# Bias tables written to DRAM once instead of once per query, and read by one overlapping read in the weights' queue

## What is computed

```python
# first block, 8 heads, causal T5 buckets
bias = rel_bias[_t5_bucket(jnp.maximum(dist, 0))]
logits = logits + bias.astype(jnp.float32)
# second block, 8 heads, a clipped relative table
bias = rel_table[:, jnp.clip(rel, -REL_CLIP, REL_CLIP) + REL_CLIP]
sc = sc + bias[:, None].astype(jnp.float32)
# second block, 4 heads, T5 buckets of both signs
bias = t5_table[:, t5_bucket(key_pos[None, :] - q_pos[:, None])]
sc = sc + bias[None, :, None].astype(jnp.float32)
```

## Time and profile before

| | |
|---|---|
| median of 3 runs | 1163.42 us (1161.92 to 1164.56) |
| span of the profiled execution | 1164.8 us |
| TensorE matmul busy | 1100.0 us, 94% |
| VectorE busy | 667.0 us, 57% |
| ScalarE busy | 555.4 us, 48% |
| GpSimd busy | 195.8 us, 17% |
| DRAM read, written | 184.94 MB, 4.98 MB |

### The profile page before, as it was taken

The page is one execution under the profiler, slowest core; times in us unless marked ns, Lnnn a source line. Parts: engine busy times, 40 slices in busy tenths (PEclk is TensorE's granted clock), DMA queues, the critical chain, the costliest instruction groups (busy, mean ns, idle before and its releaser), DMA issues.

```text
span 1164.8 us, 22065 instructions
## 1 busy us (share of the span) xinstructions
PE 1100.0 (94%) x8802; PEld 1077.8 (93%) x8802; DVE 667.0 (57%) x772; ACT 555.4 (48%) x755; POOL 195.8 (17%) x234
## 2 busy tenths in 40 slices
PE   8737699999999999999999999999999999999998
PEld 6736699999999999999999999999999999999998
DVE  4032789756587666445864444575666577544343
ACT  4121355983465444445653334454656455333343
POOL 2000011011332112103241121110000042311110
PEclk7858799999999999999999999999999999999999
DMA  6655444566467664465667644676334545865363
GB/s 212 103 117 108 135 145 127 175 211 203 141 176 216 181 181 132 140 189 193 195 172 203 182 126 136 194 236 211 115 114 142 179 145 146 219 184 167 110 191 104
DMA packets 292291, 190.93 MB, mean 164 GB/s; under 512 B 6703, under 2 KB 288866, under 8 KB 292226
## 3 DMA queue, kind: packets, MB, share of 16 engines
q1 hardware_dynamic: 286942, 183.38, 53.0%
q10 hardware_dynamic: 5284, 6.62, 3.7%
HBM read 184.94 MB, written 4.98 MB: 163 GB/s over the span
## 4 chain that ended last, share of the span: by engine, by line
PE 78%; DMA 8%; DVE 5%; ACT 4%; issue 2%; POOL 1%; ACTq 1%; SPq 0%; DVEq 0%
PE bank L1581 48%; PE bank L1561 7%; PE bank L1563 7%; PE bank L1562 7%; DMA raw<-in_w_in 4%; DMA table<-table 3%; DVE wl L1073 2%; ACT wh L474 2%; DVE page_y L1099 2%; POOL xl L955 1%; PE bank L1804 1%; PE bank L1647 1%; ACTq L551 1%; PE bank L1859 1%; PE bank L1639 1%
## 5 line engine op out<-in xcount | busy, mean ns | idle before, releaser
L1073 DVE TENSOR_TENSOR wl<-raw,wh 128x2048 fp32r<-128x2048 f32 (+3 forms) x211 | 403.1, 1911 | 328.8 <-ACT wh L474 325.7
L474 ACT ACTIVATE wh<-raw 128x2048 fp32r<-128x2048 f32 (+3 forms) x212 | 336.2, 1587 | 270.5 <-PE bank L1581 120.2
L1581 PE MATMUL bank<-xh,wh 128*128 128x256 f32 x1552 | 445.1, 287 | 7.5 <-DVE page_g L1445 4.1
L1581 PE MATMUL bank<-xl,wh 128*128 128x256 f32 x1584 | 445.5, 285 | 1.2 <-POOL xl L955 1.2
L1581 PE MATMUL bank<-xh,wl 128*128 128x256 f32 x1552 | 441.4, 285 | 0.0
L1581 PEld LDWEIGHTS bank<-xh,wh 128*128 128x128 f32 x1552 | 300.7, 194 | 9.8 <-DVE wl L1073 8.6
L1581 PEld LDWEIGHTS bank<-xl,wh 128*128 128x128 f32 x1584 | 304.7, 194 | 2.1 <-POOL xl L955 1.6
L1581 PEld LDWEIGHTS bank<-xh,wl 128*128 128x128 f32 x1552 | 300.6, 194 | 0.0
L1561 PE MATMUL bank<-hh,wh 128*128 128x256 f32 x768 | 218.7, 285 | 1.7 <-ACT page_y L680 1.6
L1563 PE MATMUL bank<-hh,wl 128*128 128x256 f32 x768 | 217.3, 283 | 0.0
L1562 PE MATMUL bank<-hl,wh 128*128 128x256 f32 x768 | 217.3, 283 | 0.0
(11 more groups left out here) (229 smaller groups left out, 975.4 us busy)
## 6 DMA issues: line engine op xcount, KB each, us to landing
raw<-in_ffn_w_in SPq DMA_DIRECT2D x88, 512.0 KB
raw<-in_w_in SPq DMA_DIRECT2D x24, 1024.0 KB
raw<-in_w_up SPq DMA_DIRECT2D x48, 512.0 KB
raw<-in_w_mix_in SPq DMA_DIRECT2D x20, 1024.0 KB
raw<-in_ffn_w_out SPq DMA_DIRECT2D x32, 448.0 KB
raw<-in_w_down SPq DMA_DIRECT2D x24, 512.0 KB
raw<-in_ffn_w_out SPq DMA_DIRECT2D x16, 512.0 KB
raw<-in_w_attn_br SPq DMA_DIRECT2D x4, 1024.0 KB
```

The source lines that it names most:

```text
L474: act.activation(wh[:, u % RING, 0:w], raw[:, u % RING, 0:w], ACT.Copy).then_inc(rounded, 1)
L1073: dve.tensor_tensor(wl[:, s, 0:w], raw[:, s, 0:w], wh[:, s, 0:w].bitcast(F32), ALU.subtract).then_inc(rest, 1)
L1581: ins = mm(lin[group(u) % 3][:, s * T:(s + 1) * T], w, (low if j == 1 else high)[:, t0 + k, :], start=(k == 0 and j == 0), stop=(k == K - ...
```

## The change

The queries of each block of 128 are kept in reverse order from the projection to the output of the attention. With query 127-p in partition p, its bias begins p values into the table's row, so partition p, head h, key t needs the word at p + 384 h + t: one read with a partition step of one word, over rows that overlap, from a table that is in DRAM once.

```diff
-        table1 = nc.dram_tensor("table1", (8, P, REL), F32).ap()
+        table1 = nc.dram_tensor("table1", (8, REL), F32).ap()
...
+            def shifted(tab, nh):
+                return bass.AP(tab.tensor, tab.offset, [[1, P], [REL, nh], [1, T]])
...
+                if name == "V":
+                    sp.wait_ge(table_out[0], 16)
+                    sp.dma_start(bias8[:, :, :], shifted(table1, 8)).then_inc(bias_in[0], 16)
+                    sp.wait_ge(clip_ready, 1)
+                    sp.dma_start(table2, clip_table).then_inc(table_out[1], 16)
...
             load(U["RI1"], gates(1))
+            sp.wait_ge(table_out[1], 16)
+            sp.wait_ge(logit_done, 6)
+            sp.dma_start(bias8[:, :, :], shifted(table2, 8)).then_inc(bias_in[1], 16)
...
+                if name == "WO":
+                    sp.wait_ge(table_out[2], 16)
+                    sp.wait_ge(lru_m2, 2)
+                    sp.dma_start(bias4[:, :, :], shifted(table3, 4)).then_inc(bias_in[2], 16)
...
-            act.activation(kidx[0:72, :], lin[0][0:72, 0:T], ACT.Copy).then_inc(read_a, 1)
-
+            act.activation(kidx[0:64, :], lin[0][0:64, 0:T], ACT.Copy)
+            act.activation(by_half(widx), backwards(lin[0][64:72, 0:T]), ACT.Copy).then_inc(read_a, 1)
+            act.wait_ge(read_a, 1)
+            act.dma_start(kidx[64:128, :], kidx[0:64, :]).then_inc(ki_twice, 16)
             act.wait_ge(tab_mm, 1)
-            act.activation(table[:, :], turn_bank[0:8, 0:REL], ACT.Copy).then_inc(tab_sb, 1)
-            act.wait_ge(tab_sb, 1)
-            act.dma_start(table1, per_query(table[:, :])).then_inc(tab_out, 16)
+            act.activation(table[:, 0, :], turn_bank[0:8, 0:REL], ACT.Copy).then_inc(tab_sb, 1)
+            act.wait_ge(tab_mm, 2)
+            act.activation(table[0:4, 1, :], o_bank[0:4, 0:REL], ACT.Copy).then_inc(tab_sb, 1)
+            act.wait_ge(tab_sb, 2)
+            act.dma_start(table1, table[:, 0, :]).then_inc(table_out[0], 16)
+            act.dma_start(table3, table[0:4, 1, :]).then_inc(table_out[2], 16)
...
-            act.wait_ge(tab_out, 16)
-            act.dma_start(bias8[:, :, :], shifted(table1, 8)).then_inc(bias_in[0], 16)
...
-            act.dma_start(table3, per_query(table[0:4, :])).then_inc(tab_out, 16)
-            act.wait_ge(clip_ready, 1)
-            act.dma_start(table2, per_query(clip_table)).then_inc(tab_out, 16)
...
-                act.activation(turned[:, t % 2, :], turn_bank[:, :], ACT.Copy).then_inc(pt_done, 1)
+                act.activation(by_half(turned[:, t % 2, :]), backwards(turn_bank[:, :]), ACT.Copy).then_inc(pt_done, 1)
```

More of the change, by code:

```diff
@@ L207, in build @@
         hrms = sb("hrms", [P, 8])
-        table = sb("table", [8, REL])
+        table = sb("table", [8, 2, REL])
         banks = [ctx.enter_context(nc.psum_tensor(f"bank{i}", [P, 512], F32)) for i in range(8)]
@@ L216, in build @@
         fin_banks = [banks[0], banks[1], banks[2], banks[5]]
-        table1 = nc.dram_tensor("table1", (8, P, REL), F32).ap()
-        table2 = nc.dram_tensor("table2", (8, P, REL), F32).ap()
-        table3 = nc.dram_tensor("table3", (4, P, REL), F32).ap()
+        table1 = nc.dram_tensor("table1", (8, REL), F32).ap()
+        table2 = nc.dram_tensor("table2", (8, REL), F32).ap()
+        table3 = nc.dram_tensor("table3", (4, REL), F32).ap()
         xtok = page_x[:, :, :].rearrange("p k t -> p (k t)").rearrange("p (i d) -> p i d", i=2)
@@ L230, in build @@
         kidx = vals[:, 1536:1792]
+        widx = vals[64:72, 1792:2048]
         decay = vals[:, 512:1536].rearrange("p (m t) -> p m t", m=4)
@@ L266, in build @@
         p_turned, p_ready = sem("p_turned"), sem("p_ready")
-        tab_mm, tab_sb, tab_out, clip_loaded, clip_ready = sem("tab_mm"), sem("tab_sb"), sem("tab_out"), sem("clip_loaded"), sem("clip_ready")
+        tab_mm, tab_sb, clip_loaded, clip_ready = sem("tab_mm"), sem("tab_sb"), sem("clip_loaded"), sem("clip_ready")
+        table_out = [sem(f"table_out{i}") for i in range(3)]
         bias_in = [sem(f"bias_in{i}") for i in range(3)]
@@ L435, in _, with backwards, by_half @@
             sp.wait_ge(stored, 64)
[L437 to L443, removed]
+        def backwards(view):
+            ap = [list(d) for d in view.ap]
+            step, n = ap[-1]
+            return bass.AP(view.tensor, view.offset + (P - 1) * step, ap[:-1] + [[P * step, n // P], [-step, P]])
+        def by_half(view):
+            ap = [list(d) for d in view.ap]
+            step, n = ap[-1]
+            return bass.AP(view.tensor, view.offset, ap[:-1] + [[P * step, n // P], [step, P]])
         def ob_raw(t, squared=False):
@@ L540, in _ @@
             act.activation(wi_s[:, :], stat_bank[:, 0:16], ACT.Copy, scale=8 ** -0.5).then_inc(wi_ready, 1)
-            act.dma_start(kidx[64:128, :], kidx[0:64, :]).then_inc(ki_twice, 16)
             round_unit(3)
-            evac(1, qidx[:, 0:2, :])
-            act.wait_ge(tab_out, 16)
-            act.dma_start(bias8[:, :, :], shifted(table1, 8)).then_inc(bias_in[0], 16)
-            act.wait_ge(tab_mm, 2)
-            act.activation(table[0:4, :], o_bank[0:4, 0:REL], ACT.Copy).then_inc(tab_sb, 1)
-            act.wait_ge(tab_sb, 2)
-            act.dma_start(table3, per_query(table[0:4, :])).then_inc(tab_out, 16)
-            act.wait_ge(clip_ready, 1)
-            act.dma_start(table2, per_query(clip_table)).then_inc(tab_out, 16)
+            evac(1, by_half(vals[:, 512:1024]), backwards(lin[1][:, :]))
             round_unit(4)
-            evac(2, qidx[:, 2:4, :])
+            evac(2, by_half(vals[:, 1024:1536]), backwards(lin[2][:, :]))
             def qk_raw(n, g, dst):
@@ L559, in qk_raw @@
                     act.wait_ge(hstat, n - 1)
-                act.activation(logit[:, 2 + n % 2, :], lin[g % 3][:, :], ACT.Square).then_inc(hsq, 1)
-                evac(g, dst)
+                src = backwards(lin[g % 3][:, :]) if n else by_half(lin[g % 3][:, :])
+                act.activation(by_half(logit[:, 2 + n % 2, :]), src, ACT.Square).then_inc(hsq, 1)
+                evac(g, by_half(dst), src)
             def head_root(n, bank, w):
@@ L624, in _ @@
             round_unit(7)
-            qk_raw(1, 5, page_q[:, 0:2, :])
+            qk_raw(1, 5, page_q[:, 0:2, :].rearrange("p a t -> p (a t)"))
             relu(4)
@@ L895, in _ @@
                         act.wait_ge(lo_done, LO["N4"] + POOL_LOWS)
-                    evac(g, page_y[:, 2 * (e - 6):2 * (e - 6) + 2, :])
+                    dst = page_y[:, 2 * (e - 6):2 * (e - 6) + 2, :].rearrange("p a t -> p (a t)")
+                    if e < 8:
+                        evac(g, by_half(dst), backwards(bank[:, :]))
+                    else:
+                        evac(g, dst)
                 else:
@@ L1483, in _ @@
             ffn_up("UP1", H1, 0, "H1", True, 1)
+            mask_bias(1, bias8)
+            mask_bias(2, bias4)
             ffn_down("DN1", 1.0)
@@ L1509, in _ @@
                 dve.wait_ge(mm_done, g + 1)
-                dve.tensor_tensor(page_q[:, 2 * e:2 * e + 2, :], lin[g % 3][:, :].rearrange("p (s t) -> p s t", s=2),
-                                  root[:, T:2 * T].unsqueeze(1).to_broadcast([P, 2, T]), ALU.mult).then_inc(read_d, 1)
+                for s in range(2):
+                    ins = dve.tensor_tensor(by_half(page_q[:, 2 * e + s, :]), backwards(lin[g % 3][:, s * T:(s + 1) * T]),
+                                            backwards(root[:, T:2 * T]), ALU.mult)
+                ins.then_inc(read_d, 1)
             dve.wait_ge(bias_masked, 2)
```

21 lines of the change are left out of this document (8 added, 13 removed).

## The result

The changed kernel took **1102.88 us** (median of 4 runs, 1102.12 to 1103.15) against 1163.11 us for the kernel before (median of 4, 1161.92 to 1164.56): ratio 0.948, 95% interval 0.9468 to 0.9492, a gain of 60.2 us. The mechanism can be checked step by step, and so can the 6 us.

A forecast was written before the change was run, and what follows sets the result against it. Slow 128-fold table writes, stalling ScalarE and the weight loads, were taken as the bound. 56.1 - 2 + 0.4 - 0.3 = 54.2 us gain, off the 1163.4 median, gave 1109.2 us; range 1103 to 1128.

The forecast's parts named there:

- Step 1: ScalarE's stalls at table writes go: unit 3 rounded at 31 to 33 us, not 41.13; TensorE ends unit 2 at 43.2.
- Step 2: TensorE's work from 43.2 us to attend(0) sums to 65.3 us, so attend(0) could begin at 108.5, 56.1 us earlier.
- Step 3: VectorE's in-order list before attend(0), with index scores ahead of unit 8's rest, takes 2 us off the gain (0 to 10).
- A chain through VectorE between units 7 and 11 with TensorE idle: Sign, in the stretch before attend(0), that the forecast of a 2 us loss to VectorE's list is wrong.
- The first rival: VectorE's list or TensorE's lower clock holds attend(0) at 115 to 125 us; time 1113 to 1128; chance 0.25.
- Steps 4 and 5: Bias reads in SyncE's queue, before unit 5, GB0 and WO0: cost 0 under cover; ScalarE's fewer issues gain 0.4 us.
- Steps 6 and 7: ScalarE's reversed reads counted 0 (bound 17 us), extra QA products 0.3 us; two memsets moved into VectorE's idle time, cost 0.
- step 8: Behind attend(0), the work and its order are the same and all shifts.
- 1.4 above the median: In the sum, the traced span of before, 1164.8 us, was set 1.4 above the median 1163.4, giving 1109.2.
- The weights were late for another reason: Rival: loads up to attend(0) stay slow, only ScalarE's stalls go; gain 29 us, time 1134; chance 0.05.
- the overlapping read is slow: Rival: 128 partitions reading the same 12 KB hold the weights' queue; at 25 GB/s the time is 1177; chance 0.03.
- Gain above 59, if the clock or the loads help more than counted: Case of a gain beyond the forecast's 50 to 59 us; chance 0.05.

The follow-up runs named there:

- b_pool_first2: Kernel before, with one wait added: VectorE writes its first-norm low parts only after GpSimd's five are done; 1162.32 us.
- extra_reads: Changed kernel with VectorE waiting for GpSimd's low parts, plus three more overlapping table reads (2.5 MB) ahead of unit 5's load; 1106.10 us.
- reads_in_act: Changed kernel with the three bias reads and the write of the second table back in ScalarE's list; 1107.99 us.
- fan_one_act: Changed kernel plus one unused 128-fold table write (1024 rows of 1.5 KB from 8 partitions) in ScalarE's queue, not waited for until the end; 1123.77 us.
- a_again2: The changed kernel, unchanged, measured and traced again; 1102.64 us over six runs.
- pool_first2: Changed kernel with one wait added: VectorE writes its first-norm low parts only after GpSimd's five are done; 1104.47 us.
- reads_act_pf2: Changed kernel with bias reads and second table's write back in ScalarE's list, and VectorE waiting for GpSimd's low parts; 1102.68 us.
- fan_wide_pf: Changed kernel with VectorE waiting for GpSimd's low parts, plus an unused write of 1024 rows of 1.5 KB, eight from each of 128 partitions; 1103.42 us.
- fan_all_pf: Changed kernel with VectorE waiting for GpSimd's low parts, plus all three 128-fold writes (2560 rows), unused, issued by ScalarE, none waited for; 1167.48 us.

## Why the prediction was right in kind and short by 6 us

*Step 1, the stalls.* Right: rounding of unit 3 at 30.87 (forecast 31 to 33), and no stop before it. Its last sentence, that TensorE ends unit 2 at 43.2, is **the step that failed**. I took that time over from the traced execution of before. It had the toss in it: 2.8 us of idle time, and then the lower clock, under which unit 1 began at 30.00 and units 1 and 2 took 13.2 us. In the changed kernel they began at 24.31 and took 11.8, so unit 2 ended at 36.1: 5.7 and 1.4 us sooner, 7.1 in all. In before only 2.75 us of it reach attend(0), as `b_pool_first2` shows; the three DMA pieces that I meant to remove filled the chain of waits, and I did not look ahead of them.

*Step 2, the work left.* Right: forecast 65.3 us, measured 101.58 - 36.1 = 65.5, with the stop of 0.58 us in it. Only TensorE's start was wrong, not its list.

*Step 3, VectorE.* Forecast 2 us, measured the 0.58 us between units 8 and 9 (79.28 to 79.86). The place was right, behind unit 8; the size was 1.4 too large. A chain through VectorE between units 7 and 11 with TensorE idle was named as a sign of being wrong, and in this small size it came. The first rival, a new bound there, did not come: clock 1.00, TensorE never short of work for long.

*Steps 4 and 5, the reads.* Right. SyncE issued the first at 28.94 and unit 5 at 29.87, and they landed in 5.7 to 7.4 us. I had put unit 5 at 33. On the rule that step 4 takes from the Trainium skill (page "DMA: Bandwidth & Descriptors", section "How a descriptor splits into AXI transactions"), that a row off a 256-byte boundary costs more, no run here shows such a cost: `extra_reads` moved 2.5 MB of such rows at some 270 GB/s, and by the records of its packets from 29.5 to 44 us a 1 KB row took 46 ns (median), the same as in the changed kernel from 216 to 245 us, where the rows of `w_out` begin on whole kilobytes.

*Steps 6 and 7, the reversed reads and the memsets.* Right: 597 ns against 598, and the memsets stand where VectorE still idles (0.16 us before them, 1.12 behind). VectorE of the changed kernel:

```profile
412.26 0.76 DVE L1375 MEMSET bias<- 64x512 f32 x2 [0.16 <-issue]
414.14 2.36 DVE L1092 TENSOR_TENSOR wl<-raw,wh 128x1024 fp32r<-128x1024 f32 x2 [1.12 <-ACT wh L495]
```

*The sum.* At attend(0), the forecast was 164.65 - 54.2 = 110.4 and the trace has 101.6. The 8.9 us are 7.1 from the start and 1.8 from step 3, the 0.4 of issues and the small terms. Behind attend(0) the span is another 0.9 us shorter (999.2 against 1000.15), where step 8 had no difference: 9.8 in all, a span of 1100.8 against the forecast 1110.6. In the times only 6.0 of them appear, and this is the second half of the same mistake: I took the gain, read from an execution with the toss, off the median of runs. In every run that shows both, the time is 1.8 us above its span, so the traced execution of before stands for about 1166.6 us (an estimate from its 1164.8), 3.5 above the median; "1.4 above the median" compared a span with times. The two halves have opposite signs, and that the error is 6 us and not 9.8 is luck. Before's own toss is worth 2.75 us at attend(0). Like for like the forecast held better: from `reads_in_act`, whose trace has the toss too, attend(0) came at 106.68 with unit 1 begun at 27.35; begun at 30.00 as before it would be 109.3 by my estimate, against 110.4.

*The rivals.* "The weights were late for another reason" falls with `fan_one_act`, "the overlapping read is slow" with `extra_reads`. "Gain above 59, if the clock or the loads help more than counted" is what happened, by the clock in part; it had a chance of 0.05 and should have had more, since a trace of before with a clock of 0.65 in one stretch could only err on that side.

*Open.* Why the toss falls as it does was not tested beyond its removal, nor what spreads the runs of one kernel by 2 to 3 us beside it. The traces show one thing that goes with it: the lower clock comes without the toss too. In `a_again2`, `pool_first2`, `reads_act_pf2` and `fan_wide_pf` GpSimd's five took 3.5 to 3.7 us, and yet the first matmuls of unit 1 ran at the lower clock, to 25.4 to 27.4 us, against 31.8 to 34.3 in the four traces with the slow toss; in the trace of the result, at 1.00, there was none of it. In `a_again2` unit 1 began 1.4 us earlier than there, and attend(0) came at the same time, 101.56. What makes the clock fall there was not tested.

## To carry to other kernels

Do not copy data by DMA out of a few partitions many times over, even if nobody waits for it: where the addresses allow it, write it once and let an overlapping read replicate it. In a forecast, ask of every starting time that is taken over from the old trace whether anything depended on it there; work that was hidden keeps its delays unseen, and the change brings them into the open. Before summing, look at the granted clock and the stretches ahead of the first changed instruction, and compare the traced execution with the median of the runs.

## What was unexpected of the hardware

- 1024 rows of 1.5 KB took about 221 ns each from 8 partitions (each row 128 times) and 65 ns each from 128, and the 221 ns rows left the weights' queue beside them 33 GB/s (40 to 50 us of `fan_one_act`). The Trainium skill, page "DMA: Bandwidth & Descriptors", section "Why a DMA increments its semaphore by 16 and not by 1", says that the outermost dimension decides how many engines share a transfer. With 8 rows outermost that would be half of them, and the DMA share of 0.45 in the earlier trace rows agrees; it does not explain the time of a row.
- ScalarE, issuing a DMA while some 1000 rows of its queue were still to be written, was held: 10.91 and 10.59 us, 4.83 and 37.31 us in `fan_all_pf`. The first such write, with nothing ahead of it, was issued in 0.82 us (`fan_one_act`).
- Two instructions of VectorE and GpSimd, 40 to 60 ns apart, decide about 5 us of the changed kernel's time from run to run. In the trace of before more went to the clock that TensorE lost than to the wait itself: of the 5.7 us by which unit 1 is late, 3.0 are idle time, 0.2 an earlier difference and the other 2.5 the lower clock, which took 1.4 more in units 1 and 2.
- Reading PSUM with a step of -1 costs ScalarE nothing (597 ns for 512 columns).
